# A decoder layer on one core: output and down projections with tokens on the partitions, the second norm by token tiles, its modulation rows formed early on the vector engine

## What is computed

```
mod = silu(c) @ w_ada + b_ada          # six rows of 1024: shift1, scale1, gate1, shift2, scale2, gate2
h = rms_norm(x, g1) * (1 + scale1) + shift1
q, k, v, qi, ki, wi, u, g_attn, g_pool = split(h @ w_in)
attn = sparse attention over the 128 keys with the highest indexer score
merged = sigmoid(g_attn) * (attn @ w_attn_br) + sigmoid(g_pool) * (pool(u) @ w_pool_br)
x = x + gate1 * (merged @ w_out)
h2 = rms_norm(x, g2) * (1 + scale2) + shift2
y = conv3(h2 @ w_up) + conv_b;  a, b = split(y)
x = x + gate2 * ((silu(a) * b) @ w_down)
```

## Time and profile before

| | us |
|---|---|
| median of three runs | 775.0 |
| lowest and highest | 772.53, 775.78 |
| the profiled execution | 773.41 |
| its span in the profile | 771.7 |
| PE busy in the span | 747.6 |
| DVE, ACT, POOL busy | 377.5, 308.3, 357.6 |

### The profile page before, as it was taken

The page is one execution under the profiler, slowest core; times in us unless marked ns, Lnnn a source line. Parts: engine busy times, 40 slices in busy tenths (PEclk is TensorE's granted clock), DMA queues, the critical chain, the costliest instruction groups (busy, mean ns, idle before and its releaser), DMA issues.

```text
span 771.7 us, 9535 instructions
## 1 busy us (share of the span) xinstructions
PE 747.6 (97%) x3618; PEld 603.4 (78%) x3618; DVE 377.5 (49%) x682; ACT 308.3 (40%) x496; POOL 357.6 (46%) x187
## 2 busy tenths in 40 slices
PE   4989999999989999999999999999999999999997
PEld 3367788787868788888777888888888888888886
DVE  2572499954756873558936344555343443000000
ACT  4234423437666653333235434343434343222121
POOL 1135368346656483455943444443444443444250
PEclk9979999999999999999999999999999999999999
DMA  8933113231043343546654333233323332233401
GB/s 327 371 112 110 55 54 89 77 107 30 28 164 110 110 149 125 183 144 199 220 216 131 108 110 107 69 98 110 95 72 107 110 95 74 79 107 96 130 21 55
DMA packets 94461, 91.72 MB, mean 119 GB/s; under 512 B 2003, under 2 KB 85711, under 8 KB 94415
## 3 DMA queue, kind: packets, MB, share of 16 engines
q1 hardware_dynamic: 92239, 82.71, 34.1%
q10 hardware_dynamic: 2176, 8.39, 3.2%
HBM read 89.00 MB, written 2.10 MB: 118 GB/s over the span
## 4 chain that ended last, share of the span: by engine, by line
PE 83%; DVE 9%; DMA 3%; SPq 2%; issue 1%; ACT 1%; ACTq 0%; DVEq 0%
PE bank L1373 48%; PE bank L1382 24%; DVE work L1156 2%; DVE top L1153 2%; PE bank L1404 2%; DMA ada<-in_w_ada_dram 2%; DVE macc L1045 2%; PE bank L1628 1%; PE bank L1607 1%; PE bank L1595 1%; PE bank L1463 1%; PE bank L1409 1%; SPq L514 1%; DMA ada_mid<-in_w_ada_dram 1%; PE bank L1518 1%
## 5 line engine op out<-in xcount | busy, mean ns | idle before, releaser
L589 POOL TENSOR_TENSOR wsplit<-stage,wsplit 128x1024 fp32r<-128x1024 f32 (+2 forms) x127 | 288.7, 2278 | 367.1 <-ACT wsplit L700 367.1
L1373 PE MATMUL bank<-hT,wsplit 128*128 128x512 f32 x1200 | 286.9, 391 | 0.0
L1373 PEld LDWEIGHTS bank<-hT,wsplit 128*128 128x128 f32 x1200 | 223.7, 188 | 46.5 <-issue 0.4
L700 ACT ACTIVATE wsplit<-stage 128x1024 fp32r<-128x1024 f32 (+2 forms) x127 | 125.6, 991 | 301.7 <-PE bank L1382 288.9
L1382 PE MATMUL bank<-hT,wsplit 128*128 128x512 f32 x600 | 149.9, 392 | 0.0
L1382 PEld LDWEIGHTS bank<-hT,wsplit 128*128 128x128 f32 x600 | 111.5, 188 | 23.7 <-issue 0.6
L1373 PE MATMUL bank<-guT,wsplit 128*128 128x512 f32 x352 | 84.0, 390 | 0.0
L1373 PEld LDWEIGHTS bank<-guT,wsplit 128*128 128x128 f32 x352 | 65.8, 188 | 13.6
L1335 DVE SCALAR_TENSOR_TENSOR yb<-bank,conv,yb 128x511 f32<-128x511 f32 (+1 forms) x44 | 33.0, 749 | 66.0 <-ACT yb L967 65.2
L1335 DVE SCALAR_TENSOR_TENSOR ya<-bank,conv,ya 128x511 f32<-128x511 f32 (+1 forms) x44 | 33.0, 749 | 60.1 <-ACT ya L967 59.4
L1360 DVE SCALAR_TENSOR_TENSOR xT<-bank,mod,xT 128x512 f32<-128x512 f32 x8 | 6.0, 751 | 111.5 <-PE bank L1382 111.5
(11 more groups left out here) (182 smaller groups left out, 814.2 us busy)
## 6 DMA issues: line engine op xcount, KB each, us to landing
stage<-in_w_up_dram SPq DMA_DIRECT2D x44, 512.0 KB, 5.1
stage<-in_w_in_dram SPq DMA_DIRECT2D x17, 1024.0 KB, 5.2
ada_mid<-in_w_ada_dram ACTq DMA_DIRECT2D x8, 1024.0 KB, 5.3
stage<-in_w_down_dram SPq DMA_DIRECT2D x8, 1024.0 KB, 5.3
ada<-in_w_ada_dram SPq DMA_DIRECT2D x7, 1024.0 KB, 12.3
stage<-in_w_ada_dram SPq DMA_DIRECT2D x4, 1024.0 KB, 5.2
stage<-in_w_out_dram SPq DMA_DIRECT2D x4, 1024.0 KB, 6.8
ada_last<-in_w_ada_dram SPq DMA_DIRECT2D x4, 1024.0 KB, 8.4
```

The source lines that it names most:

```text
L589: pool.tensor_tensor(unit_split(n, 1), unit_source(n), unit_split(n, 0).bitcast(F32), ALU.subtract).then_inc(low, 1)
L700: me.did(act.activation(unit_split(n, 0), unit_source(n), ACT.Copy), high)
L1373: pe.matmul(out_bank[:, :], hi[:, k, :], rhs[:, part, k0 + k, :], start=first and k == 0 and part == 0, stop=False)
```

## The change

The output and down projections are turned round: the activation tile (128 features x 128 tokens) is the stationary operand and 512 columns of the weights move, so that results have tokens on the partitions. `block_rows` cuts their weights into units of 2 x 128 rows by 512 columns, `tile_products` does six matmuls of one unit for one token tile. x stays as it came (`xtok`), the residual is added there, and the output is stored from it without a transpose. The gates are needed along the free dimension: `gate_sums` makes both halves of a gate row on all partitions with two fp32 matmuls of 512 columns, `gate_vector` adds the bias. The output projection is done in two column halves. In the first, all four token tiles grow together; in the second, one tile after the other is finished, with its own weight places (`own`), and the second norm of a tile starts: squares with a sum along the row, root, scaling by it (`xs`), transposes back on PE (`x2_turn`), scale and shift (`h2_full`), high and low part. The first four up units are done for the first 256 tokens, then for the second. Rows 3 and 4 of the modulation are made by DVE from the end of the first norm to the first top-k round, from loads of their own (`ada_early`), row 2 by DVE during ab and wo. POOL makes no row any more. `keep_clock` is gone. The down projection has two column halves of 11 pairs, each for four token tiles.

```diff
 ROW_LOADS = 11
+ROW_TURN = {1: 0, 3: 1, 4: 2, 2: 3, 5: 4}
...
+    def block_rows(self, w, k0, k1, half, home=None):
+        item = self.stage(w, (half * S,), k0, k1, NT)
+        for part in range((k1 - k0) // 2):
+            self.units.append((2, part, S))
+            self.house(home and home(k0 // 2 + part))
+            self.item_of.append(item)
+            self.last_use[item] = ("unit", len(self.units))
+            self.unit[w, half, k0 // 2 + part] = len(self.units) - 1
...
+        if at is None:
+            banks = NBANK - 1 if name in FILLERS else NBANK
+            at = self.ring = (self.ring + 1) % banks
+        self.before.append(max((k for k in range(n) if self.bank[k] == at), default=None))
+        self.bank.append(at)
...
-    for n, name in enumerate(FILLERS):
+    for name in FILLERS:
         s.product(*name)
-        if n % 4 == 3:
-            s.mod(2, n // 4)
...
+    for half in range(2):
+        for k0 in range(0, KD, 4):
+            s.block_rows("out", k0, k0 + 4, half, (lambda n: ("own", n)) if half else None)
+        for t in range(NT):
+            s.opens(("wo", half, t), "dve", (3 + t, None)[half] if not half or t < NT - 1 else 3)
...
         item = s.stage("up", (m * P, FF + m * P), 0, KD, 1)
         for part, kind in enumerate(("ua", "ub")):
...
+            last = (kind, m) == ("ub", 1)
+            s.split(item, part, (kind, m), ("own", 2) if last else None)
+            s.opens((kind, m), "dve", 3 if last else None)
...
+    for half in range(2):
+        for k0 in range(0, KF, 4):
+            s.block_rows("down", k0, min(k0 + 4, KF), half)
+        for t in range(NT):
+            s.opens(("dn", half, t), "dve", (3 + t, None)[half] if not half or t < NT - 1 else 7)
...
+            def load_early(j, q):
+                sp.wait_ge(mod_sum, KD if j == 3 else KD * ROW_TURN[3] + 2 * q + 2)
+                if j == 3 and q == 0:
...
+                sp.dma_start(ada_early[q][:, :, :], ada[:, 2 * q:2 * q + 2, j * D:(j + 1) * D]
...
             for n, item in enumerate(sch.items):
+                if n == NSTAGE:
+                    for q in range(KD // 2):
+                        load_early(3, q)
+                if n in (NSTAGE + 3, NSTAGE + 4):
+                    for q in (2 * (n - NSTAGE - 3), 2 * (n - NSTAGE - 3) + 1):
+                        load_early(4, q)
                 if item[:3] == ("w", "up", (3 * P, FF + 3 * P)):
-                    sp.wait_ge(used, sch.unit["wo", KD - 1] + 1)
+                    sp.wait_ge(x2_ok, 2 * NT)
+                    sp.dma_start(gate_row[:, :], b_ada[0:1, 5 * D:6 * D].to_broadcast([P, D])).then_inc(gate_in, 16)
                     for q in range(KD // 2):
                         load_last(q)
...
-            def mod_rows(j, q):
...
-                    if k == 0:
-                        pool.tensor_tensor(macc[:, :], row, c_k, ALU.mult).then_inc(mod_sum, 1)
-                    else:
-                        pool.tensor_tensor(row, row, c_k, ALU.mult).then_inc(mod_term, 1)
-                        pool.wait_ge(mod_term, k)
-                        pool.tensor_tensor(macc[:, :], macc[:, :], row, ALU.add).then_inc(mod_sum, 1)
...
-            for n, name in enumerate(FILLERS):
-                through(name)
-                if n % 4 == 3:
-                    mod_rows(2, n // 4)
-            for m in range(1, KD - 1):
-                low_parts(min(sch.unit["wo", m] + 3, sch.unit["wo", KD - 1] + 1))
-                pool.wait_ge(x2_sq, m + 1)
-                if m > 1:
...
+            high_parts(sch.unit["out", 1, NT - 1] + 1)
...
+            def square_half(half, t):
+                act.wait_ge(x2_ok, half * NT + t + 1)
+                if half or t:
...
+                me.did(act.activation(junk2[:, :], xtok[:, t, half * S:(half + 1) * S], ACT.Square,
+                                      accum_out=tstat[:, half, t:t + 1]), x2_sq)
...
+            def scaled(t):
+                act.wait_ge(x2_inv, t + 1)
+                if t >= 2:
+                    act.wait_ge(xs_t, 2 * (t - 1))
+                for half in range(2):
+                    cols = slice(half * S, (half + 1) * S)
+                    me.did(act.activation(xs[:, t % 2, cols], xtok[:, t, cols], ACT.Copy, scale=tstat[:, 3, t:t + 1]),
+                           xs_ok)
...
+            me.did(act.activation(tstat[:, 2, 0:1], ones[:, 0:1], ACT.Sqrt))
+            for t in range(NT):
+                square_half(0, t)
+            high_parts(sch.unit["ua", 1])
+            square_half(1, 0)
+            token_root(0)
+            scaled(0)
+            high_parts(sch.unit["ua", 1] + 1)
+            for t in (1, 2):
+                square_half(1, t)
+                h2_high(t - 1, 0)
+                token_root(t)
+                h2_high(t - 1, 1)
+                scaled(t)
+            square_half(1, NT - 1)
+            token_root(NT - 1)
+            scaled(NT - 1)
+            high_parts(sch.unit["ub", 1] + 1)
+            for t in (NT - 2, NT - 1):
+                for half in range(2):
+                    h2_high(t, half)
...
-            norm(0, 0)
+            norm()
+            mod_rows(3, 0)
+            mod_rows(3, 1)
...
             for m in range(2):
                 dve.wait_ge(part_hi, m + 1)
                 low_of(qiT[:, 1, m, :], bank(("qi", m))[:, :], qiT[:, 0, m, :], drained["dve"])
+            mod_rows(3, 2)
+            mod_rows(3, 3)
...
                 for k in index_steps(n)[3:]:
                     index_sum(k)
+                mod_rows(4, n)
...
+            mod_vector(3)
...
+            mod_vector(4)
...
-            mod_vector(2)
...
                 if m in (1, 3):
-                    mod_rows(3, m // 2)
+                    mod_rows(2, m // 2)
             merged_low(KD - 1)
-            mod_rows(3, 2)
...
+            mod_rows(2, 2)
+            mod_rows(2, 3)
+            gate_vector(0)
...
+            def residual(n, half, t, done, waits, into, signal):
+                cols = slice(half * S, (half + 1) * S)
+                dve.wait_ge(done, waits)
+                me.did(dve.tensor_tensor(into[0], banks[sch.bank[sch.chunk[n, half, t]]][:, :], gate_row[:, cols],
+                                         ALU.mult), drained["dve"])
+                me.settle()
+                me.did(dve.tensor_tensor(into[1], into[0], xtok[:, t, cols], ALU.add), signal)
...
+            def h2_full(t, half):
+                dve.wait_ge(xs_t, 2 * t + half + 1)
+                for k in range(half * KD // 2, (half + 1) * KD // 2):
+                    me.did(dve.tensor_scalar(full[:, t % 2, k, :], TURN[t % 2][half][:, k % 4 * P:(k % 4 + 1) * P],
+                                             gs[:, 1, k:k + 1], mod[:, 3 * KD + k:3 * KD + k + 1],
+                                             ALU.mult, ALU.add), full_ok if k % 4 == 3 else None)
...
+            wo_residual(1, 0)
+            token_sum(0)
+            token_inverse(0)
+            for t in (1, 2):
+                wo_residual(1, t)
+                h2_full(t - 1, 0)
+                token_sum(t)
+                h2_full(t - 1, 1)
+                token_inverse(t)
+                h2_low(t - 1)
+            wo_residual(1, NT - 1)
+            token_sum(NT - 1)
+            token_inverse(NT - 1)
+            for t in (NT - 2, NT - 1):
+                h2_full(t, 0)
+                h2_full(t, 1)
+                h2_low(t)
...
+            def tile_products(n, out_bank, rows_of, t, k0, first, last):
+                pe.wait_ge(high, n + 1)
+                pe.wait_ge(low, n + 1)
+                for r in range(sch.units[n][0]):
+                    for a, b in THREE:
+                        mm = pe.matmul(out_bank[:, :], rows_of[:, a, k0 + r, t * P:(t + 1) * P],
+                                       unit_split(n, b)[:, r, :], start=first and r == 0 and (a, b) == THREE[0],
+                                       stop=last and r == 1 and (a, b) == THREE[-1])
+                return mm
...
             product(("u", 0), hT)
             squares(KA - 1)
+            mod_columns(3)
             for g in range(1, KA):
                 product(("u", g), hT)
+                if g == 1:
+                    mod_columns(4)
...
+            for pair in range(NT):
+                pe.wait_ge(m_lo, 2 * pair + 2)
...
-            for m in range(KF):
-                if m == 0:
-                    first_products((("ua", 0), ("ub", 0)), 1, 0)
...
+                    name = ("wo", 0, t)
+                    if pair == 0:
+                        await_tile_bank(name)
+                    mm = tile_products(sch.unit["out", 0, pair], bank(name), merged, t, 2 * pair, pair == 0,
+                                       pair == NT - 1)
+                    if t == NT - 1:
+                        mm.then_inc(used, 1)
+                    elif pair == NT - 1:
+                        mm.then_inc(wo_done, 1)
+                if pair == NT - 2:
+                    await_bank(pe, ("wo", 1, 2))
```

(43 more changed lines are left out.)

460 lines of the change are left out of this document (213 added, 247 removed).

## The result

The changed kernel took 766.12 us in the median of four executions (764.18 to 768.33), the kernel before 775.39 beside it: ratio 0.9897, 95% interval 0.9875 to 0.9919, so 9.3 us or 1.0% faster. The forecast was 762.5, in a range from 757.5 to 769.5. So the gain in the medians is nearer 7 us than 9. The profiled execution took 764.18 us with a span of 762.4, against 773.41 and 771.7.

The account below looks back on a forecast made before the run. PE was taken as the bound, busy 747.6 of 771.7 us. Terms +3.1 -3.0 -1.7 -7.3 -2.4 -0.5 = -11.8 took 773.4 to 761.6; splitting the difference to the median base gave 762.5 us, range 757.5 to 769.5.

Parts of the forecast that it names:

- Bound, and full-width products: Whole kernel: PE is the bound; 512-column matmuls stay at 227 ns; down projection -2.4 us as output transposes go.
- Half-width matmuls: First four up units: 192 matmuls of 256 columns at 120 ns, 23.0 us; straight line from transposes gives 142 ns.
- The rival that ends slower: First four up units: 256-column matmuls cost up to a full one's 227 ns, 43.6 us, time 783; chance 0.05.
- Token chain: Second norm: DVE and ACT take about 4.1 us a token tile, PE 5.44; tile 1 comes 0.4 to 0.8 late.
- The rival by which the clock falls in the second norm: Second norm: without clock-holding matmuls PE is granted less, about 4 us lost plus 2 of waiting, time 768.5; chance 0.15.
- First gate: Output projection: row 2 needed after 72 matmuls, at 345 + 16.3; DVE done at 358 to 362, covered or 1 us late.
- Column sum at the end of attention: End of attention: PE's column sum of row 2 goes, -1.7 us.
- Early rows: Before the top-k rounds: sixteen row operations move to DVE, which comes 3.1 us later: +3.1, bounds 2.6 and 7.
- The rival of row operations in the way: Early stretch: DVE's rows meet POOL's low parts, top-k starts 6 to 7 us late, time 766.5; chance 0.20.
- Attention: Attention: POOL's row operations and four 1 MB loads go, taking back 3.0 of 3.6 us idle; bounds 0 and -3.6.
- End: Kernel end: two DVE operations and a store replace transposes, ACT's copy and a store: -0.5 us, bounds 0 and -1.
- Base and median: Base: profiled execution 773.4 gives 761.6, 1.6 below the median base of 775.0; difference split, forecast 762.5.

Follow-up runs that it names:

- the quarters: Changed kernel with each token half of the first four up units cut once more, into matmuls of 128 columns: 785.07 us, ratio 1.0142.
- the kernel without waits: Changed kernel with row 2's third operation pair after the sixth merge and the first branch product taken row block by row block: 759.19 us, ratio 0.9815.
- branch product split: Changed kernel with the first branch product row block by row block, nine matmuls before the wait for the last heads: 766.23 us, ratio 0.9903.
- no halves: Changed kernel with the first four up units over all 512 tokens, after the last transposes: 779.15 us, ratio 1.0067.
- Later gate sums: Changed kernel with the first gate's two sums after all 96 matmuls of the first column half instead of 72: 762.43 us, ratio 0.9864.

## Why the prediction was right, and where it was off

The measured 766.1 us lie inside the range, and the parts that make the gain came as said; two terms did not.

**Bound, and full-width products.** Right. PE stayed the bound, up changed by 0.1 us, and the down projection lost 2.6 (2.4 said).

**Half-width matmuls.** Right, 120 ns as taken. The estimate next to the load's 106 was the good one, the straight line's 142 the bad one; the quarters show why. The rival that ends slower needed 185. The two gate sums took 1.3 to 1.4 us, not 1.7.

**Token chain.** "0.4 to 0.8 us too late" for the first half: it was not late, not even in the kernel without waits. What the halves hide was measured by taking them away, 13 us. The rival by which the clock falls in the second norm did not come true there: 1.00 from 343.69 on in the profile, transposes included, so the rule of the Trainium skill (TensorE: Matmul & The Clock Gate, PE-mode transpose) that a transpose does not count as a busy PE changed nothing here.

**First gate.** DVE "needs four 1.27 us operations, 2.19 when POOL is working: 358 to 362. Covered, or 1 us late." This step failed. DVE was free when I said, 8.0 us into the stretch, and PE arrived when I said; but the operations took 11.3 us and not 5.1 to 8.8, and PE waited 2.96. I had taken the median of the earlier trace rows as the price beside POOL, where their maximum is 3.3, and had not carried over that the change itself, with four places of their own for the weights, makes POOL run without a pause just there. Two operations of one column took only 2.0 of it away, and a row pair moved into DVE's idle time all of it. The stretch took 75.45: 71.9 of work, as the run without waits shows, 2.96 of this wait and 0.6 that its seams lost besides; I had 71.4 and 1.0.

**Column sum at the end of attention.** "The column sum of row 2 at its end goes too: -1.7." This step failed too. It brought 0.4: the product behind it waits for DVE's low part of the last head anyway. Cutting the sum in the kernel before brought nothing either.

**Early rows.** +3.1 said, +2.7 measured, near the lower bound of 2.6. I said that the later of DVE and PE decides, and took DVE. In the profile PE reached the third v transpose at 141.03 without a wait, so PE's two column sums decided. The rival of row operations in the way was close, though: two more operations, and 4.36 us are lost.

**Attention.** -3.0 said, -3.3 measured. The cause I named, the queue, is that of one wait only; taken away by itself it brought 1.0, so the right size is in part luck.

**End.** -0.5 said, -1.1 measured, 0.2 of which is how the two marks are taken (start of the transposes, end of a matmul). The rest is small: DVE's last operation ends 1.5 us behind the last product, where the transposes and the copy took 2.3.

**Base and median.** The terms were summed against one execution, and that one was near the long-run median of before (773.5), so the 0.9 us that I added for the base was for nothing, and made up for part of what was missed. Its counterpart was 764.18, 2.6 above the sum of 761.6, and the median 1.9 higher again. The mean granted clock, which every execution has, points to what those 1.9 are: of the 51 executions of before beside the experiments, 32 have 0.993 and take 773.3 us in the mean, and 13 have 0.989 or less and take 775.6. Of the changed kernel's eight, the one at 764.18 has 0.992 and the other seven, 766.0 to 768.3, have 0.990 or less. So its executions lose to the lower clock more often than those of before, and the medians show 7 us where the two profiles show 9. My forecast had no term for that. That a lower mean clock is such falls is seen in the profiled executions only, so this part stays an argument.

## What to carry to other kernels

A piece of work that stands just ahead of a wait may be free, and taking it out then brings only the wait; look at when the next engine delivers before crediting it. Price a DVE operation beside a busy GpSimd by what GpSimd will do after the change, not by the median of what it did before; making such an operation narrower saves little, and moving it away from the last deadline, into a stretch in which DVE had been idle, saves the wait. Cutting a product into token halves to cover a latency chain costs little as long as a matmul keeps the 256 columns that its weight load hides here.

## What I had not expected of the hardware

A wait of 3 us, or 1.9 us of one-column matmuls without any wait, is at times followed by the lower clock level for about 3 us, which costs 1.6; behind the wait of 4.36 us it was about 5. It came in four of nine profiles behind the same instruction, and behind the 2.96 us gate wait in two of six (branch product split, no halves). So removing a wait of 3 us can bring 4.5 in some executions and 3 in others. Later gate sums brought 3.7 in the median where the profile's stretch shows 1.8. Three of its four executions (762.09 to 762.66) have a mean clock of 0.993, and against the changed kernel's one execution without a fall behind the first 56 us, 764.18, they are 1.5 to 2.1 us shorter, as the stretch is. The rest of the 3.7 is then likely falls in the changed kernel's other executions; it is not shown, since one execution of each run was profiled.

A DVE operation of one column took 2.2 and 2.3 us beside a GpSimd that subtracts without a pause, against 0.15 elsewhere.
